# Two PSUM arrangements of a hybrid decoder trunk: projections in the score banks, three transpose banks

## What is computed

```python
h = split_cols(x @ w_in)                       # queries, keys, values, gates
decay = jnp.transpose(jnp.cumsum(logf, axis=1), (0, 2, 1))
out_a = causal_dense_attention(qa, ka, va, key_valid, HEAD_DIM ** -0.5, decay)
out_b = mla_attention(h['b_cq'], h['b_ckv'], h['b_kr'], g_q, g_kv, w_uq, w_ukv, pos, key_valid)
out_c = dsa_sparse_attention(..., h['c_iq'], h['c_ik'], h['c_iw'], key_valid, rel_bias, top_k)
out_d = sliding_window_sink_attention(...)
mixed = jnp.concatenate([out_a * jax.nn.silu(h['a_g']), ..., out_d * jax.nn.silu(h['d_g'])], axis=-1)
y = mixed @ w_out
return layer_norm(ALPHA * x + y, ln_g, ln_b)
```

## Time and profile before

| what | value |
|---|---|
| median of 3 runs | 3140.01 us (3136.19 to 3141.57) |
| the profiled execution, its own time | 3137.17 us |
| span of its trace | 3135.4 us |
| PE busy | 2948.5 us, 94% of the span |
| PE weight loads | 1721.4 us, 55% (beside the products) |
| DVE busy | 1711.5 us, 55% |
| ACT busy | 990.4 us, 32% |
| POOL busy | 550.1 us, 18% |
| mean granted clock of PE | 0.988 |

### The profile page before, as it was taken

How to read it: one execution, slowest core, us unless ns; L and a number is a source line. 1 busy time by engine, 2 the same in 40 slices (tenths; PEclk the granted TensorE clock), 3 DMA queues, 4 the chain that set the end, 5 groups by cost and what they waited for, 6 DMA issues and landing times. The chain is left out here.

```text
span 3135.4 us, 40420 instructions
## 1 busy us (share of the span) xinstructions
PE 2948.5 (94%) x14358; PEld 1721.4 (55%) x14358; DVE 1711.5 (55%) x4569; ACT 990.4 (32%) x2965; POOL 550.1 (18%) x946
## 2 busy tenths in 40 slices
PE   7999999998899999999999999999988999998998
PEld 5446666554455666644544466665545556665443
DVE  5338877766776444412233388877667764444222
ACT  3233333333444333300012333333334443333000
POOL 1002222111111133300000022221111111333000
PEclk9999999999999999999999999999999999999999
DMA  5101111101000021042120011111110001210421
GB/s 212 54 14 38 41 48 36 33 25 50 16 15 18 22 90 44 15 143 80 54 86 28 14 38 47 47 31 33 31 46 14 16 16 31 93 31 24 151 78 42
DMA packets 89103, 152.70 MB, mean 49 GB/s; under 512 B 10640, under 2 KB 66592, under 8 KB 86856
## 3 DMA queue, kind: packets, MB, share of 16 engines
q1 hardware_dynamic: 88904, 150.12, 14.6%
HBM read 120.12 MB, written 32.08 MB: 49 GB/s over the span
## 5 line engine op out<-in xcount | busy, mean ns | idle before, releaser
L1027 PE MATMUL ps_s<-xT,w_ring 128*128 128x348 f32 (+4 forms) x3616 | 1132.7, 468 | 10.8 <-DVE arena L1377 4.8
L1027 PEld LDWEIGHTS ps_s<-xT,w_ring 128*128 128x128 f32 x3616 | 678.5, 193 | 396.4 <-issue 105.9
L1635 POOL TENSOR_SCALAR arena<-arena,small 128x1040 f32<-128x1040 f32 (+8 forms) x544 | 353.3, 661 | 1495.0 <-DVE small L1548 1493.7
L1257 ACT ACTIVATE arena<-arena,small 128x1040 f32<-128x1040 f32 (+8 forms) x544 | 369.4, 679 | 174.0 <-DVE small L1536 173.5
L1268 ACT ACTIVATE arena<-ps_t 16x32 f32<-16x32 f32 (+4 forms) x940 | 285.2, 353 | 348.4 <-PE ps_t L1094 342.4
L1298 DVE MAX8 small<-score 128x8 f32<-128x1040 f32 (+6 forms) x448 | 376.4, 840 | 10.5
L1094 PE MATMUL ps_t<-ident,arena 128*128 128x128 f32 (+2 forms) x2400 | 348.9, 277 | 33.1 <-DVE arena L1500 17.6
L1300 DVE MATCH_REPLACE8 score<-small,score 128x1040 f32<-128x1040 f32 (+6 forms) x448 | 369.8, 826 | 0.0
L1094 PEld LDWEIGHTS ps_t<-ident,arena 128*128 128x128 f32 (+2 forms) x2400 | 252.0, 132 | 155.5 <-issue 80.1
L1071 PE MATMUL ps_s<-feat 64*128 64x256 f32 (+13 forms) x1824 | 305.0, 437 | 29.6 <-DVE small L1536 24.1
L1106 PE MATMUL ps_o<-arena 128*64 128x256 f32 (+3 forms) x3136 | 282.3, 320 | 24.2 <-ACT cT L1192 14.8
(11 more groups left out here) (148 smaller groups left out, 2280.3 us busy)
## 6 DMA issues: line engine op xcount, KB each, us to landing
w_ring<-in_w_feat SPq DMA_DIRECT2D x78, 512.0 KB, 3.6
mixed<-mixg SPq DMA_DIRECT2D x128, 128.0 KB, 1.7
feat<-mixed SPq DMA_DIRECT2D x16, 1024.0 KB, 6.6
resid<-score SPq DMA_DIRECT2D x16, 512.0 KB, 3.1
score<-resid SPq DMA_DIRECT2D x16, 512.0 KB, 7.6
arena<-in_w_out SPq DMA_DIRECT2D x4, 1536.0 KB, 8.1
cT<-falls SPq DMA_DIRECT2D x8, 520.0 KB, 4.8
feat<-falls SPq DMA_DIRECT2D x8, 520.0 KB, 5.3
```

Source lines behind the costliest of these rows:

```text
L1027: mm = pe.matmul(ps_s[:, bank, 0:w], w_ring[:, wt % 2, k, :], xT[:, k, c0:c0 + w], start=(k == 0), stop=(k == KT - 1))
L1257: nc.scalar.activation(p, p, ACT.Exp, scale=-1.0, bias=nm[:, e:e + 1], accum_out=psums[0:M, st % 4, e:e + 1]).then_inc(S["exp_done"], 1)
L1635: nc.gpsimd.tensor_scalar(p, p, rinv[0:M, st % 4, e:e + 1], 1.0, ALU.mult, ALU.mult).then_inc(S["nrm_done"], 1)
```

## The change

Bank 4 of the scores is given to the transposes. `ps_s` has four banks, `ps_t` three (`T_BANKS`), and `bank_left` waits for the copy of the group three back. A projection has no bank of its own: `group` takes the next slot from `next_slot`, of which it uses the first bank, so that projections and chunks of scores take turns in the two slots. The token projections between the layers take the bank of the output projection that is not in use; `k_latent` uses banks of the two slots. The first output projection begins in bank `yh % 4`, and its first two pieces are no longer put into the last two steps of branch C.

```diff
-P_BANK = 4
+T_BANKS = 3
...
     def group(self, by, bank):
 
+        bank = self.next_slot() if bank is None else bank
         g, k = self.take("pj"), self.take("pj_" + by)
         return dict(g=g, bank=bank, free=self.banks([bank], ("pj_" + by, k + 1)), nth=k + 1)
...
-    def token_block(self, l, what, b, bank=P_BANK):
+    def token_block(self, l, what, b, bank=None):
...
-        bank = P_BANK if b == ORDER[0] and half == 0 else yh % 4
+        bank = yh % 4
...
-    def chunk(self, l, wt, what, c, bank=P_BANK, **kw):
+    def chunk(self, l, wt, what, c, bank=None, **kw):
...
-                                                **self.group("act" if what == "N" else "dve", P_BANK))
+                                                **self.group("act" if what == "N" else "dve", None))
...
-        for c, bank in enumerate((free, P_BANK, 2 - free)):
+        for c, bank in enumerate((free, free + 1, 2 - free)):
...
-                self.token_block(l + 1, "TC", blocks[idx - 2])
+
+                self.token_block(l + 1, "TC", blocks[idx - 2], bank=(2 * self.n["yy"] + 1) % 4)
...
-                    self.add("cum", l=l, cum=cum, waits=self.banks([P_BANK], ("cum_free", cum + 1)))
+                    bank = self.next_slot()
+                    self.add("cum", l=l, cum=cum, bank=bank, waits=self.banks([bank], ("cum_free", cum + 1)))
...
             put(5, lambda: self.add("yl", l=l, b=ORDER[0], yy=yy, ln=None))
-            for idx in (7, 8):
-                put(idx, lambda: self.y_parts.pop(0)())
...
-        ps_s = ctx.enter_context(nc.psum_tensor("ps_s", [BLK, 5, 512], F32))
-        ps_t = ctx.enter_context(nc.psum_tensor("ps_t", [BLK, 2, 512], F32))
+        ps_s = ctx.enter_context(nc.psum_tensor("ps_s", [BLK, 4, 512], F32))
+        ps_t = ctx.enter_context(nc.psum_tensor("ps_t", [BLK, T_BANKS, 512], F32))
...
-            if tg >= 2:
-                if by_act[tg - 2]:
-                    eng.wait_ge(S["t_act"], act_upto[tg - 1])
+            if tg >= T_BANKS:
+                n = tg - T_BANKS + 1
+                if by_act[n - 1]:
+                    eng.wait_ge(S["t_act"], act_upto[n])
                 else:
-                    eng.wait_ge(S["t_dve"], tg - 1 - act_upto[tg - 1])
+                    eng.wait_ge(S["t_dve"], n - act_upto[n])
```

More of the change, by code:

```diff
@@ L169, in __init__ @@
                       yy=0, cn=0, tri=0, nb=0, ds=0)
-        self.bank_owner = [None] * 5
+        self.bank_owner = [None] * 4
         self.row_owner = [None] * 3
@@ L182, in __init__ @@
             if idx >= 2:
-                self.token_block(0, "TC", ORDER[idx - 2], bank=idx % 5)
+                self.token_block(0, "TC", ORDER[idx - 2], bank=idx % 4)
         self.add("pro", l=0, waits=self.banks([1, 2], ("line_ready", 1)))
@@ L738, in copies @@
             for first, rows, heads, k, h0, col, step, M in runs:
-                src = ps_t[0:rows, tg % 2, 0:heads * per * BLK].rearrange("p (e c t) -> p e c t", e=heads, c=per)
+                src = ps_t[0:rows, tg % T_BANKS, 0:heads * per * BLK].rearrange("p (e c t) -> p e c t", e=heads, c=per)
                 src = src[:, :, first:first + k, it["M"] - M:it["M"]]
@@ L969, in _ @@
                             k = 4 * j + c
-                            mm = pe.transpose(ps_t[:, tg % 2, c * BLK:c * BLK + M],
+                            mm = pe.transpose(ps_t[:, tg % T_BANKS, c * BLK:c * BLK + M],
                                               x_new[0:M, it["ln"] % 2, k * BLK:(k + 1) * BLK], ident[0:M, 0:M])
@@ L1007, in _ @@
                     for j in range(3):
-                        mm = pe.transpose(ps_t[:, tg % 2, j * BLK:j * BLK + M],
+                        mm = pe.transpose(ps_t[:, tg % T_BANKS, j * BLK:j * BLK + M],
                                           cn[0:M, it["cn"] % 2, j * BLK:(j + 1) * BLK], ident[0:M, 0:M])
@@ L1017, in _ @@
                     for k, src in ((5, upper1[:, 0:BLK]), (3, upper1[:, BLK:2 * BLK])):
-                        mm = pe.matmul(ps_s[0:NB * NH, P_BANK, 0:BLK], fw[:, k, :], src, start=(k == 5), stop=(k == 3))
+                        mm = pe.matmul(ps_s[0:NB * NH, it["bank"], 0:BLK], fw[:, k, :], src, start=(k == 5), stop=(k == 3))
                     mm.then_inc(S["cum_full"], 1)
@@ L1093, in _ @@
                             k0, w = key_cols(it["br"], i, kb)
-                            mm = pe.transpose(ps_t[0:w, tg % 2, c * BLK:c * BLK + M], p_row(it, h, k0, w),
+                            mm = pe.transpose(ps_t[0:w, tg % T_BANKS, c * BLK:c * BLK + M], p_row(it, h, k0, w),
                                               ident[0:M, 0:M])
@@ L1149, in _ @@
                     for k in range(4):
-                        a = nc.scalar.activation(xT[:, k, tok0(b):tok0(b) + M], ps_t[:, tg % 2, k * BLK:k * BLK + M],
+                        a = nc.scalar.activation(xT[:, k, tok0(b):tok0(b) + M], ps_t[:, tg % T_BANKS, k * BLK:k * BLK + M],
                                                  ACT.Identity, scale=gains[:, l + 1, k:k + 1],
@@ L1191, in _ @@
                         gain = gq[:, 2 * l + j:2 * l + j + 1] if j < 2 else gkv[:, l:l + 1]
-                        a = nc.scalar.activation(cT[:, j, BLK * b:BLK * b + M], ps_t[:, tg % 2, j * BLK:j * BLK + M],
+                        a = nc.scalar.activation(cT[:, j, BLK * b:BLK * b + M], ps_t[:, tg % T_BANKS, j * BLK:j * BLK + M],
                                                  ACT.Copy, scale=gain)
@@ L1200, in _ @@
                     act.wait_ge(S["line_stored"], 32)
-                    nc.scalar.activation(falls_sb, ps_s[0:NB * NH, P_BANK, 0:BLK], ACT.Copy, scale=-1.0
+                    nc.scalar.activation(falls_sb, ps_s[0:NB * NH, it["bank"], 0:BLK], ACT.Copy, scale=-1.0
                                          ).then_inc(S["cum_free"], 1)
@@ L1346, in _ @@
                         k = 4 + c
-                        t = dve.tensor_scalar(xT[:, k, tok0(b):tok0(b) + M], ps_t[:, tg % 2, c * BLK:c * BLK + M],
+                        t = dve.tensor_scalar(xT[:, k, tok0(b):tok0(b) + M], ps_t[:, tg % T_BANKS, c * BLK:c * BLK + M],
                                               gains[:, l + 1, k:k + 1], gains[:, l + 1, KT + k:KT + k + 1],
```

## The result

The changed kernel takes 3223.0 us (median of 4 runs, 3218.7 to 3226.5) against 3138.3 us before (4 runs, 3136.2 to 3141.6): 1.0267 times as long, 95% interval 1.0255 to 1.0279. It is slower by 85 us. The profiled execution took 3226.5 us, 89.4 us more than that of before.

A forecast was written before the change was run, and what follows sets the result against it. PE, busy 94% of the span, bounds the kernel. Per layer 61.5 us lost, 18.6 gained, 43 net, twice 86; on 3137.2 us that is 3223, and the median 2.8 above: 3226 us; 8 in 10 range 3176 to 3266.

The forecast's parts named there:

- index scores: Index stage: projections and second chunks wait for evictions of the banks they now share, 12 us a layer lost.
- branch B, waits: Branch B: second chunks wait for the late rotation, 26 us, plus gate pieces and other places; 33.5 us a layer lost.
- branch B, clock (PE's busy time): PE's clock falls to half after six of nine new waits a layer in B, 1 us each: 6 us, bounds 0 and 15.
- branch D: End of branch D: runs of projections (L990, L1036) alternate between banks and stop waiting for evictions, 6 us a layer gained.
- branch C: Branch C: ten gate pieces and second chunks wait 0.4 to 0.65 us, 5 us a layer lost; moved output-projection pieces 0.
- third transpose bank: Transposes wait for a copy one group earlier; 80% of 31.6 us of waits goes, 12.6 us a layer gained.
- rungs: Branch B: successive PE waits for the late rotation, each delay passed on through DVE; 4.4, 3.1 and 3.6 us in pair 0.
- DVE catches up: Rival, chance 0.15: in B each pair pays only its first wait, 11 us in place of 26; 3188 us.
- gate term: Branch B: gate piece after block 8's scores waits 0.65 us, the next about half; four pairs, 4.4 us.
- Nothing is taken up: Rival, chance 0.12: B's waits keep their full lateness, 31 us a layer, A 10, slow clock after all nine waits; 3264 us.
- Faster: Rival, chance 0.04: DVE draws level after one long PE stop in each branch, so gains outweigh costs; 3127 us.
- No difference: Rival, chance 0.04: banks may be free whenever asked for, leaving only small gains and losses; 3140 us.

## Why the prediction was right

The forecast was 3226 us, and the time is 3223. The mechanism was right: where the waits would stand, that DVE would hand them on, and that PE's clock would fall after them. That the sum came within 3 us is luck, since errors of up to 29 us in its terms cancelled. In both layers, in us (measured: stages of the traces; "shared" is the run with two transpose banks against before, "after" the changed kernel):

| term | predicted | shared | after |
|---|---|---|---|
| index scores | +24 | +17.2 | +17.0 |
| branch A | +10, less its part of the transposes' gain | +7.5 | +3.1 |
| branch B, waits | +67, less its part | +56.1 | +50.2 |
| branch B, clock (PE's busy time) | +12 | +39.8 | +40.6 |
| branch D | -12 | -6.7 | -5.7 |
| branch C | +10 and 0 for the moved pieces, less its part | +4.1 (with the pieces' -6.7) | -14.6 |
| third transpose bank | -25 | | -30 |

**The reading of waits that aren't there yet** held. From starts of PE and ends of evictions in the trace before, the first rungs of pair 0 were put at 4.4 and 3.1 us, and stand at 3.87 and 2.97; 18 waits of 52 to 60 us in all were forecast, and there are 18 of 50.2. That the rungs are passed on was the point on which the second rival hung ("DVE catches up", 3188 us): it falls with the timeline above, where the value products hold DVE back. Moving the top-k steps took 34 us off the rungs, which shows what they are made of.

**The clock was the term that was mis-sized**: 12 us in both layers, with a bound of 30. PE's busy time rose by 51.1 us, 40.6 us of it in B; the 10.5 us elsewhere are within the 1%, 29 us, that the forecast allowed outside B. In "a fall after six, 1 us each" the number was about right, 12 in both layers against 13 more slow stretches than before. The price was wrong: 40.6 us for 13 is 3 us each. Half of the stretches in B last twice as long as the one of the earlier trace rows, and the value products stand in the loop, so their slow part lengthens the rungs instead of lying beside them. Of the 18 waits for the rotation, 13 had a stretch at 0.50 under way at their end or within 2 us after it; the other five, one of them of 3.2 us, had none.

The rule cited from the Trainium skill (TensorE: Matmul & The Clock Gate, "HAM oscillation — how this bites in real kernels") spoke for a higher clock term, 30 us in place of 12, and the 40.6 us measured are on that side. The page tells it of a kernel with waits of some 3 to 5 us; that every wait is followed by a slow stretch, this trace does not bear out, with five of 18 that were not.

**What made up for it.** B's waits were forecast at 67 us and grew by 56.1 us without the third bank. The rotation's waits were near the forecast, 51.6 us, but L1036's waits for the rotation, 6.0 us before, are gone, which leaves 46 where 52 were summed; the gate pieces and the other places take some 10 where 15 were summed. The gate term of 4.4 us a layer was also 0.5 us too high by its own rows (0.65 and half of it, four times, are 3.9). The index stage costs 17 and not 24: 9.8 us of waits and 7.2 us of PE's busy time, which the forecast did not have there. The projections wait 9.8 us for index evictions in 28 places (0.35 us each), where 44 places at 0.4 were taken. And the 2.5 us a layer for DVE's additions were no new wait. PE had waited for the same additions before, at the next chunk, which the earlier trace rows do not show; first before, then after:

```profile
PE ps_s L1053 <- DVE arena L1409: 3.9, 2, 2.0
```

```profile
PE ps_s L1055 <- DVE arena L1411: 4.2, 2, 2.1
```

The moved pieces give 6.7 us and not 0: the wait for w_out before was a wait with nothing to do in it, and they stand in it now. The third transpose bank gives 30 us and not 25; the waits for copies stay gone almost whole. On the other side, branch D gave half of its 12. PE's waits in D did fall by 10.6 us, although one kind of wait there (L992, for the rotation) grew from 7.0 to 9.2 us, but PE's busy time in D rose by 4.9 us, with the granted clock at 0.97 in both layers where it was 0.98 and 0.99. In the run that changes the end of D alone, PE is not slower there and the 12 us are whole.

**The rivals.** "Nothing is taken up", 3264 us, had a clock term of 31 us, nearer to the 40.6, but the rungs too long (50 us of waits, not 62). "Faster" asked that the waits for DVE and the clock stay under 13 us a layer, 26 in both; with 50.2 + 16.3 + 15.3 us of them and 40 us of clock it is out. "No difference" is out too.

## What to carry to other kernels

When a bank, a buffer or a queue is to be shared, take the start of each user in the old trace and the end of the work that will release it: the difference is the new wait, and it must then be followed through the engine that releases it, because what stands behind the waiting instruction may be what that engine needs next. A long wait of PE can cost more than its length: here the 18 waits of 1.6 to 3.9 us (50.2 us) brought 40.6 us of slower work with them, and the same 18 waits at 1.0 us and less brought almost none. So couple PE to an engine that runs late only where the release is near. The bank was worth giving away stage by stage: transposes need it in branch C, projections in B. The kernel that hands it over for C is 0.5% faster than the kernel before, the moved pieces included, and 1% faster with the two queues at the end of D.

## What the runs showed of the hardware that was not expected

A slow stretch of TensorE followed waits that were partly filled: with 14 transposes (1.75 us) in each of 18 waits and 24.2 us left in 16 of them, the granted clock of B was still 0.96; with 2.8 us of products in each (51.2 in 18) and 8.2 us left, 0.97 and 0.98, that of the kernel before. The 14 transposes put behind the waits raised nothing: the kernel's mean clock was 0.975, against 0.977 with no fill. And with the waits cut to 1.0 us at most by less work of DVE in these steps, without any fill, B was granted 0.99 and 0.98.
